# A two-layer hybrid decoder trunk in split float32: other addresses for the weight buffers, x, the normed x and the split activations

## What is computed

```python
for l in range(2):
    h = rms_norm(x, attn_norm_w[l])
    proj = h @ w_in[l]                       # 2048 x 4624: q, k, v, z, xBC, dt
    q, k, v, z, xbc, dt_raw = split(proj)
    attn = sliding_window_attention(q, k, v, q_norm_w[l], k_norm_w[l], sinks[l])
    ssm = mamba2_mixer(z, xbc, dt_raw, ...)   # conv, SiLU, chunked scan, gate, grouped norm
    x = x + concat([attn, ssm]) @ w_out[l]    # 2048 x 2048
    h = rms_norm(x, ffn_norm_w[l])
    x = x + (silu(h @ w_gate[l]) * (h @ w_up[l])) @ w_down[l]   # 2048 x 5632, 5632 x 2048
return x
```

## Time and profile before

| | |
|---|---|
| time, three runs | 2196.06, 2196.25, 2196.36 us |
| median | 2196.25 us |
| the profiled execution: time | 2196.58 us |
| the profiled execution: span | 2194.8 us |
| instructions in it | 25026 |
| granted TensorE clock, mean | 0.999 |
| read from HBM | 388.43 MB, 178 GB/s over the span |

### The profile page before, as it was taken

One profiled execution on the slowest core, in us unless ns is written; L12 is line 12 of the kernel. 1 busy time (PEld: TensorE's weight loads), 2 busy tenths in 40 slices (PEclk: granted clock), 3 DMA queues, 4 the chain that ended last, 5 costly groups with the idle time before them and its releaser, 6 DMA issues.

```text
span 2194.8 us, 25026 instructions
## 1 busy us (share of the span) xinstructions
PE 2181.9 (99%) x10142; PEld 1794.2 (82%) x10150; DVE 1176.0 (54%) x1382; ACT 1001.2 (46%) x1292; POOL 112.9 (5%) x157
## 2 busy tenths in 40 slices
PE   9999999999999999999999999999999999999999
PEld 7888788888888888888888888888888888888887
DVE  5856665445544554444467667554544454444443
ACT  5555654444444444443445556444444444443332
POOL 2023100000000000000000222000000000000000
PEclk9999999999999999999999999999999999999999
DMA  7554356666666665555555543566666666656553
GB/s 216 175 168 127 117 175 183 192 193 190 190 183 194 190 191 186 185 185 185 186 165 178 156 129 126 181 177 195 189 188 192 190 189 189 190 186 197 196 195 126
DMA packets 202850, 392.16 MB, mean 179 GB/s; under 512 B 12224, under 2 KB 12592, under 8 KB 202736
## 3 DMA queue, kind: packets, MB, share of 16 engines
q1 hardware_dynamic: 201952, 388.67, 57.7%
q0 software_dynamic: 784, 1.90, 0.4%
HBM read 388.43 MB, written 2.10 MB: 178 GB/s over the span
## 4 chain that ended last, share of the span: by engine, by line
PE 98%; ACT 1%; issue 0%; POOL 0%; SPq 0%; DMA 0%; DVE 0%; DVEq 0%; ACTq 0%
PE ps L484 91%; PE ps L493 3%; PE ps L586 1%; PE ps L535 0%; PE ps L650 0%; PE ps L649 0%; PE ps L622 0%; PE ps L623 0%; PE ps L648 0%; POOL ys L451 0%; DMA vrows<-in_k_norm_w_dram 0%; PE ps L574 0%; PE ps L591 0%; PE ps L594 0%; PE ps L577 0%
## 5 line engine op out<-in xcount | busy, mean ns | idle before, releaser
L1047 DVE TENSOR_TENSOR w_lo<-raw,w_hi 128x1024 fp32r<-128x1024 f32 x736 | 906.7, 1234 | 882.4 <-ACT w_hi L807 881.3
L807 ACT CAST w_hi<-raw 128x1024 fp32r<-128x1024 f32 x736 | 772.4, 1050 | 965.0 <-PE ps L484 958.5
L484 PE MATMUL ps<-w_hi,h_hi 128*128 128x512 f32 x1984 | 622.9, 395 | 0.0
L484 PE MATMUL ps<-w_hi,h_lo 128*128 128x512 f32 x1984 | 612.3, 390 | 0.0
L484 PE MATMUL ps<-w_lo,h_hi 128*128 128x512 f32 x1984 | 611.3, 389 | 0.0
L484 PEld LDWEIGHTS ps<-w_hi,h_lo 128*128 128x128 f32 x1984 | 372.6, 188 | 78.6
L484 PEld LDWEIGHTS ps<-w_lo,h_hi 128*128 128x128 f32 x1984 | 372.4, 188 | 78.8
L484 PEld LDWEIGHTS ps<-w_hi,h_hi 128*128 128x128 f32 x1984 | 366.1, 188 | 70.9 <-DVE w_lo L1047 0.7
L484 PE MATMUL ps<-w_hi,f_hi 128*128 128x512 f32 x960 | 304.6, 398 | 0.0
L484 PE MATMUL ps<-w_hi,f_lo 128*128 128x512 f32 x960 | 302.7, 396 | 0.0
L484 PE MATMUL ps<-w_lo,f_hi 128*128 128x512 f32 x960 | 302.7, 396 | 0.0
(11 more groups left out here) (183 smaller groups left out, 819.7 us busy)
## 6 DMA issues: line engine op xcount, KB each, us to landing
raw<-in_w_gate_dram SPq DMA_DIRECT2D x176, 512.0 KB, 4.4
raw<-in_w_up_dram SPq DMA_DIRECT2D x176, 512.0 KB, 3.8
raw<-in_w_down_dram SPq DMA_DIRECT2D x176, 512.0 KB, 3.6
raw<-in_w_in_dram SPq DMA_DIRECT2D x144, 512.0 KB, 3.6
raw<-in_w_out_dram SPq DMA_DIRECT2D x64, 512.0 KB, 3.6
out_dram<-xr SPq DMA_DIRECT2D x4, 512.0 KB, 5.2
xr<-in_x_dram POOLq DMA_DIRECT2D x3, 512.0 KB, 5.9
xr<-in_x_dram SPq DMA_DIRECT2D x1, 512.0 KB, 4.4
```

The lines of the kernel that those rows point to most:

```text
L484: done = nc.tensor.matmul(ps[:, bank + t, :], lhs[:, rows + k, t * P:(t + 1) * P], w[:, slot, k, :], start=(first and k == 0 and w is w_hi ...
L807: nc.scalar.copy(w_hi[:, slot, :, :], raw[:, slot, :, :]).then_inc(hi_split, 1)
L1047: v_.tensor_tensor(w_lo[:, slot, :, :], raw[:, slot, :, :], w_hi[:, slot, :, :].bitcast(F32), ALU.subtract).then_inc(lo_split, 1)
```

## The change

It gives `sb` an alignment and asks for 512 bytes for `raw`, `w_hi`, `w_lo`, `xr`, `h_hi` and `h_lo`. It rounds the home of `f_hi` down to a multiple of 1024, and takes `sp` and `dtx` (used by the softplus of dt) out of the row of small buffers and puts them behind `f_lo`. No instruction is added, removed or moved in order.

```diff
-        def sb(name, shape, dt=F32):
-            return ctx.enter_context(nc.sbuf_tensor(name, shape, dt))
+        def sb(name, shape, dt=F32, align=32):
+            return ctx.enter_context(nc.sbuf_tensor(name, shape, dt, align_bytes=align))
...
-        raw = sb("raw", [P, RING, 2, N])
-        w_hi = sb("w_hi", [P, RING, 2, N], F32R)
-        w_lo = sb("w_lo", [P, RING, 2, N], F32R)
-
-        xr = sb("xr", [P, T, D])
-        h_hi = sb("h_hi", [P, KT, TOK], F32R)
-        h_lo = sb("h_lo", [P, KT, TOK], F32R)
+        raw = sb("raw", [P, RING, 2, N], F32, 512)
+        w_hi = sb("w_hi", [P, RING, 2, N], F32R, 512)
+        w_lo = sb("w_lo", [P, RING, 2, N], F32R, 512)
+
+        xr = sb("xr", [P, T, D], F32, 512)
+        h_hi = sb("h_hi", [P, KT, TOK], F32R, 512)
+        h_lo = sb("h_lo", [P, KT, TOK], F32R, 512)
         stage = sb("stage", [P, 2, T, N])
...
-        dtx = sb("dtx", [P, T, HS])
...
-        sp = sb("sp", [P, 6, T, HS])
...
         TILE = TOK * 4
-        at_hi = 229344 - 2 * FT * TILE
+        at_hi = (229344 - 2 * FT * TILE) // 1024 * 1024
         at_lo = at_hi + FT * TILE
         m_hi = f_hi = nc.alloc_sbuf_tensor_at("f_hi", [P, FT, TOK], F32R, offset=at_hi)
         m_lo = f_lo = nc.alloc_sbuf_tensor_at("f_lo", [P, FT, TOK], F32R, offset=at_lo)
+        sp = nc.alloc_sbuf_tensor_at("sp", [P, 6, T, HS], F32, offset=at_lo + FT * TILE)
+        dtx = nc.alloc_sbuf_tensor_at("dtx", [P, T, HS], F32, offset=at_lo + FT * TILE + 6 * T * HS * 4)
```

## The result

The changed kernel takes 2175.43 us (median of four runs, 2174.87 to 2175.83) against 2196.31 for the kernel before. The ratio is 0.9905, with a 95% interval of 0.9888 to 0.9922. The forecast was 2175.2 us. The profiled execution took 2175.55 us around a span of 2173.7.

A forecast was written before the change was run, and what follows sets the result against it. The prediction took TensorE's weight products, their number times their pace, to bound the kernel. A gain of 21.9 us less 0.4 and 0.4 made 21.1, from 2196.25 to 2175.2 us, range 2150 to 2197.

The forecast's parts named there:

- Step 1: Output and down projections: 2880 products from f or m reach h's pace at a multiple-of-64 home, gaining 21.9 us.
- Step 2: The other 5952 products, with w and h moved to multiples of 512: no change, taken as 0.
- Steps 3 and 4: Small scan and attention matmuls on buffers under f, then splits and raw loads: no effect, each taken as 0.
- Step 5: Given back: 0.4 us waiting before line 648 in the output projection, 0.4 us for slower products after breaks.
- All products faster: Rival: all 8832 products speed up because homes 128 past a multiple of 512 cost time; 2075 us, chance 0.16.
- The home isn't the cause: Rival: products from f or m are slower for another reason, so no effect; 2196 us, chance 0.10.
- The h stages lose their even pace: Rival: with w and h at multiples of 512, 5952 products slow to 234.3 ns; 2241 us, chance 0.08.

The follow-up runs named there:

- f_64: Kernel before with f_hi alone moved 32 bytes down to 139200, a multiple of 64 but not of 128: 2194.18 us, ratio 0.9991.
- f_only: Kernel before with f_hi and f_lo alone moved to multiples of 1024, w and h left in place: 2191.39 us, ratio 0.9979.
- f_128: Kernel before with f_hi and f_lo moved to 128 past a multiple of 512, like w and h: 2175.62 us, ratio 0.9906.
- h_32: Changed kernel with h_hi and h_lo alone moved 32 bytes further up: 2210.96 us, ratio 1.0066.
- h64_f256: Changed kernel with h 64 and f 256 bytes off w modulo 512: 2211.45 us, ratio 1.0068.
- h128_f192: Changed kernel with h 128 and f 192 bytes off w modulo 512: 2212.04 us, ratio 1.007.
- half_load: Kernel before with products of the low activation loading 64 of 128 stationary columns, writing 64 PSUM partitions: 2209.55 us in one run.
- all_160: Kernel before with raw, w, xr, h and f all moved to 160 past a multiple of 512: 2175.8 us, ratio 0.9906.

## Why the prediction was right

The number was right, 2175.2 against 2175.43 us, and so was the mechanism as far as it went: 2880 products change their pace because an address changed. The rule for which address it is was wrong.

- **Step 1, f and m.** 21.9 us were predicted, from 234.3 to 226.7 ns a product; both paces were measured just so. But the step blames the odd home and takes any multiple of 64 for good. f_64 and f_only refute that, with 233.3 and 232.3 ns. The change hit the right place since it brings f and w to a distance of 0 modulo 256. Of the two facts that I had about f (off a multiple of 64, and 352 bytes off w modulo 512), I made the wrong one the cause. The trace of before couldn't tell them apart by these products. That the right change followed from the wrong rule was luck: moving f to a multiple of 64 alone (f_64) gave 2 us.
- **Step 2, w and h.** 0 was right, for the reason given in passing: the distance stays what it was. The evidence from the dt products was misread. Their 113 ns at other distances was taken to say that distance doesn't matter. The stationary operand starts at 192, 320, 448 and 64 past a multiple of 512 in turn, not at 192 and 448, which is 64 and 192 off its moving operand modulo 256; at any other pair of distances in these runs the same instruction takes 118 or 119 ns. A row about another shape, whose distances happened to suit it, was carried over to 512 columns. The row of maskb proves nothing on this either: maskb and its stationary operand identb (home 123520) are 1280 bytes apart, 0 modulo 256. The step also let one think that moving w adds nothing. With f at its new home it is most of the gain: f_only, where w stays, takes 2191.39 us and the changed kernel 2175.43.
- **Steps 3 and 4.** Eight transposes of ys take 0.87 us and eight of xr 0.88 after, against 0.87 for both. Splits are at 1234 and 1049 ns, and the loads of raw landed within 0.2 us of before. At 0, as costed.
- **Step 5.** The wait before line 648 grew by 0.2 us in all, half of the 0.4 forecast. The other 0.4 us, for slower products after breaks, came to 0.6: by that much the spacings of f after sum to more than 226.7 ns each, while those before average 234.3 with their breaks.
- **All products faster** (0.16): out. With all operands at multiples of 512 the pace is 226.7 ns, as it was. The rule of the Trainium skill (TensorE: Matmul & The Clock Gate, Part 1, "Wait - 56ns, not 53.3ns?") that stood beside this rival, 215.7 ns between starts for 512 columns on the warm clock, isn't reached at any of the eight distances; at the best of them this kernel stays 11 ns above it.
- **The home isn't the cause** (0.10): out, by f_128, where f's home alone moves and the whole gain comes.
- **The h stages lose their even pace** (0.08): the loss is real, and h_32 and h64_f256 show its price, 35 to 36 us, but a common offset isn't what sets it off. The change doesn't, because h and w keep their distance. By the table, aligning w and leaving h (128 apart, as in h128_f192) would have brought it about; that kernel was not run.

What stays open: why the even pace is 226.7 ns, 32 cycles of 2.4 GHz over its 512 columns, what has a period of 256 bytes, and what picks between two paces at one distance. That the load of the next stationary operand meets the stream was my picture. The dependence on the distance fits it, also where no other engine works, but half_load, with shorter loads and no gain, doesn't bear it out, so it isn't shown. No version tried was faster than the changed kernel; f_128 equals it within the interval, with one number changed.

## What to carry to other kernels

Where TensorE streams 512 columns of float32r past a fresh stationary operand each time, look at the distance between the two operands' homes and not at either alignment. A multiple of 256 bytes was worth 2 to 8 ns of 234 on each matmul over every other distance tried, for no instruction. It is read from start-to-start times in a quiet stretch, and with two stages of different pace in one kernel it is the first thing to compare. Measure it for the shape at hand: with 256 columns another distance was better, and a mixture of loads of two lengths lost the even pace altogether. And work out the distance of every matmul in the run from the steps of both operands, as it may alternate.

## What the runs showed that I had not expected

- The pace depends on the distance of the two operands modulo 256 bytes, not on a common offset: 226.7 ns with all homes 0, 128 or 160 past a multiple of 512.
- The curve is uneven: 234.3 ns at 96, 232.3 at 128, 233.4 at 160, 228.9 at 192.
- Loading 64 columns in place of 128 in a third of the loads made 512-column products slower, 230.1 against 226.7 ns.
- The same matmul on the same homes ran at 113 ns in one kernel and at 119 in another, and at both in the two layers of half_load.
- The dt products, 256 columns, lost their 113 ns wherever h or wdt_s was moved off their first distances: 119.0 ns in all_160, where wdt_s and h are 32 bytes further apart and the products ahead have the even pace.
